# Three edits to one layer pair's kernel: first norm's root after the projections, small sums for the heads' norm, output projection begun during the retention's norm

## The reference

```
n = rms_norm(h, attn_norm_w)                 # per token: x * rsqrt(mean(x^2)+eps) * w
proj = n @ w_in                              # 1024 x 2816: aq 512, ak 128, av 128, rq, rk, rv, rg 512 each
aq = rope(rms_norm(aq per head of 64, q_norm_w)); ak = rope(rms_norm(ak per head, k_norm_w))
y_attn = windowed attention with a sink, |i-j| <= 128, 8 heads over 2 key heads
rq = rope(rq); rk = rope(rk) / 8
ret = bidirectional retention(rq, rk, rv)    # chunks of 128 tokens, decays forward and backward
y_ret = silu(rg) * rms_norm(ret per head of 64, ret_norm_w)
h = h + concat(y_attn, y_ret) @ w_out
h = h + (silu(m @ w_gate) * (m @ w_up)) @ w_down,  m = rms_norm(h)
```

## Time and profile before

| | |
|---|---|
| runs | 2897.14 us median of 3 (2895.31 to 2898.72) |
| the profiled execution | 2896.42 us, span of its instructions 2894.6 us |
| granted TensorE clock, mean | 0.986 |
| TensorE busy | 2768.2 us, 96% of the span |
| VectorE, ScalarE, GpSimd busy | 1606.4, 926.1, 1330.9 us |

### The profile page before, as it was taken

How to read it: one execution, slowest core, us unless ns; L and a number is a source line. 1 busy time by engine, 2 the same in 40 slices (tenths; PEclk the granted TensorE clock), 3 DMA queues, 4 the chain that set the end, 5 groups by cost and what they waited for, 6 DMA issues and landing times. The chain is left out here.

```text
span 2894.6 us, 36614 instructions
## 1 busy us (share of the span) xinstructions
PE 2768.2 (96%) x13748; PEld 2239.7 (77%) x13748; DVE 1606.4 (55%) x2419; ACT 926.1 (32%) x1793; POOL 1330.9 (46%) x1012
## 2 busy tenths in 40 slices
PE   5999989999999999999999899999899999999997
PEld 4777778778888888777766688878777788888886
DVE  7865665585555555542367742143368655555555
ACT  5655422232232222223334410021243322222222
POOL 3332332365656566543222234446613656566663
PEclk9999999999999999999999999999999999999999
DMA  3101001111111111131101011121201111111111
GB/s 123 37 30 37 30 20 75 50 44 55 52 60 54 48 55 52 44 117 37 37 30 38 30 37 56 53 113 62 66 23 44 48 59 55 48 55 51 59 51 66
DMA packets 71375, 151.94 MB, mean 52 GB/s; under 512 B 6448, under 2 KB 29360, under 8 KB 70064
## 3 DMA queue, kind: packets, MB, share of 16 engines
q1 hardware_dynamic: 64256, 123.76, 13.5%
q10 hardware_dynamic: 6960, 26.01, 2.3%
HBM read 141.36 MB, written 8.39 MB: 52 GB/s over the span
## 5 line engine op out<-in xcount | busy, mean ns | idle before, releaser
L603 POOL TENSOR_TENSOR WH<-WRAW,CST 128x512 fp32r<-128x512 f32 x204 | 228.1, 1118 | 896.5 <-PE PS L719 755.4
L717 PE MATMUL PS<-XH,WH 128*128 128x512 f32 x1248 | 514.7, 412 | 3.5 <-DVE XL L1994 2.8
L719 PE MATMUL PS<-XH,WL 128*128 128x512 f32 x1248 | 490.1, 393 | 0.0
L718 PE MATMUL PS<-XL,WH 128*128 128x512 f32 x1248 | 489.3, 392 | 0.0
L628 POOL TENSOR_TENSOR WL<-WRAW,WH 128x512 fp32r<-128x512 f32 x216 | 310.0, 1436 | 274.6 <-ACT WH L1622 273.6
L2377 DVE TENSOR_TENSOR H<-H,PS 128x512 f32<-128x512 f32 x352 | 235.8, 684 | 159.7 <-PE PS L1014 157.5
L717 PEld LDWEIGHTS PS<-XH,WH 128*128 128x128 f32 x1248 | 235.8, 189 | 85.7 <-issue 38.1
L1012 PE MATMUL PS<-HH,WH 128*128 128x512 f32 x704 | 275.0, 391 | 5.3 <-DVE HL L2311 5.3
L1622 ACT ACTIVATE WH<-WRAW 128x512 fp32r<-128x512 f32 x204 | 129.0, 632 | 471.5 <-PE PS L1014 383.1
L605 POOL TENSOR_TENSOR WL<-WRAW,WH 128x512 fp32r<-128x512 f32 x204 | 271.9, 1333 | 16.0
L719 PEld LDWEIGHTS PS<-XH,WL 128*128 128x128 f32 x1248 | 235.5, 189 | 51.6
(11 more groups left out here) (323 smaller groups left out, 5034.1 us busy)
## 6 DMA issues: line engine op xcount, KB each, us to landing
WRAW<-ws SPq DMA_DIRECT2D x104, 512.0 KB, 3.5
WRAW<-ws SPq DMA_DIRECT2D x176, 256.0 KB, 2.6
RAWX<-ws SPq DMA_DIRECT2D x88, 256.0 KB, 2.7
H<-xT ACTq DMA_DIRECT2D x4, 1024.0 KB, 10.9
H<-xT ACTq DMA_DIRECT2D x2, 2048.0 KB, 10.2
h_spill<-H ACTq DMA_DIRECT2D x1, 4096.0 KB, 11.8
H<-h_spill ACTq DMA_DIRECT2D x4, 1024.0 KB, 7.8
outT<-H ACTq DMA_DIRECT2D x4, 1024.0 KB, 4.4
```

Source lines behind the costliest of these rows:

```text
L603: pool.tensor_tensor(WH[:, j, c], WRAW[:, j, c], ONES[:, 0:1].to_broadcast((P, 512)), ALU.mult).then_inc(hi_split, 1)
L717: pe.matmul(out, WH[:, j, w], rh(kt), start=(n == 0), stop=False)
L718: pe.matmul(out, WH[:, j, w], rl(kt), start=False, stop=False)
L719: last = pe.matmul(out, WL[:, j, w], rh(kt), start=False, stop=(n == len(kts) - 1))
```

## The change

1. **First norm.** The input is no longer scaled by the inverse root ahead of the products. ScalarE rounds x times the gain at once (`x_highs`), VectorE makes the low part from x, gain and high part in one instruction (`x_lows`); the squares and sums stand between these. The root, inverse and spread of half 0 are asked for by TensorE inside the second half of `first_units`, those of half 1 behind it and inside slot 4. The spread inverse root is copied to SBUF (`RST`, in a part of RG not yet used), and VectorE's new `rooted1` multiplies each slot by it on the way from PSUM to `ACC`, and so frees the bank. `evacuate1` reads `ACC` in place of PSUM and no longer makes the scaled copy (the scale goes into `finish1`'s first instruction). `finish1`, and `after1` on both engines, run one slot later. In `first_units` the second unit lags three tiles behind in the first half too.
2. **Heads' norm.** `after1` on TensorE takes the squares as the stationary operand, 128 tokens at a time, and a 2-column matrix as the moving one: 4 products, result 128x8. Root and inverse work on 128x8; a new `spread1` (8 products of 128 moving columns) brings the inverse back to the heads' partitions in bank 6.
3. **Retention's norm.** The sums of the second half go into bank 4, spreads 0 to 3 alternate between banks 3 and 1 (so that a spread waits for the norm two before it, not one), and `r_sums(1)` and spreads 4 to 7 are issued inside the first half of the output projection's `first_units`, at tiles 2 and 6. ScalarE's `high` of tiles 0 to 3 go ahead of the second half's squares, the reload of x behind these; VectorE's inverse of half 1 goes behind the first half's `low`s.

```diff
-            for q in range(4):
+            act.wait_ge(vec_in, 32)
+            x_highs(0)
+            x_highs(1)
+            x_square(0)
+            x_square(1)
+            x_highs(2)
+            x_highs(3)
+            x_square(2)
+            norm_root(0, 0)
+            x_square(3)
+            nsq.n = 4
+            rst_copy(0)
...
-            norm_scale(0, V_N1)
+            x_lows(0)
+            x_lows(1)
+            x_sums(0)
+            x_sums(1)
+            x_lows(2)
+            x_lows(3)
+            x_sums(2)
+            norm_inverse(0, 0)
+            x_sums(3)
...
+                dve.tensor_tensor(ACC[:, g % 2], PS[:, bank], RST[h], ALU.mult).then_inc(free[bank], 1)
...
-                    pe.matmul(PS[:, MB], BD, XX[:, (g % 2) * HALF:(g % 2 + 1) * HALF], start=True, stop=True).then_inc(m_full, 1)
+                    for b in range(4):
+                        sq = XX[:, (g % 2) * HALF + b * P:(g % 2) * HALF + (b + 1) * P]
+                        last = pe.matmul(PS[:, MB, 2 * b:2 * b + 2], sq, BD[:, 0:P:64], start=True, stop=True)
...
+            def first_norm(h, kt):
+                if (h, kt) == (1, 0):
+                    norm_sums(0, 0)
+                if (h, kt) == (1, 3):
+                    norm_spread(0, 0)
+
+            def spread1(g):
+
+                pe.wait_ge(head_inv, g + 1)
+                if g:
+                    pe.wait_ge(proj_done, g)
+                for b in range(4):
+                    for hh in range(2):
+                        c = 60 + 8 * (g % 2) + 2 * b + hh
+                        last = pe.matmul(PS[64 * hh:64 * hh + 64, OB, blk(b)], STAT[:, c:c + 1].to_broadcast((P, 64)), IDENT,
+                                         start=True, stop=True)
...
-                    if done < g and (kt == 6 if g > 12 else kt == 7 or kt in (2, 5) and done < g - 1):
+                    if (g, kt) == (4, 2):
+                        norm_spread(0, 1)
+                    elif done < g - 1 and (kt == 6 if g > 12 else kt in (2, 5)):
                         after1(done)
                         done += 1
+                    elif kt in (4, 7) and spreads < min(done, 10):
+                        spread1(spreads)
+                        spreads += 1
...
-            r_sums(1)
-            for n in range(4, 8):
-                r_spreads(n)
...
+            def second_half(h, kt):
+
+                if (h, kt) == (0, 2):
+                    r_sums(1)
+                if (h, kt) == (0, 6):
+                    for n in range(4, 8):
+                        r_spreads(n)
...
-            for g in range(45):
-                if g:
+            for g in range(46):
+                if g == 2:
+                    norm_root(0, 1)
+                if 1 <= g < 45:
                     evacuate1(g - 1)
+                if g == 2:
+                    rst_copy(1)
...
-                if g:
-                    after1(g - 1)
+                if g >= 2:
+                    after1(g - 2)
...
+                if 1 <= g < 45:
+                    rooted1(g - 1)
                 if 0 <= s < 32:
                     soft1a(s)
-                if g:
-                    finish1(g - 1)
+                if g >= 2:
+                    finish1(g - 2)
```

More of the change, by code:

```diff
@@ L399, in prob @@
             return XX[:, 768 * (s % 2):768 * (s % 2) + 768].rearrange("p (a b) -> p a b", a=2)
+        RST = [RG[:, 3, half(h)] for h in range(2)]
+        PD, MF = [], []
+        for g in range(44):
+            PD.append((PD[-1] if PD else 0) + (KIND1[SLOTS1[g][0]] in "qkrR"))
+            MF.append((MF[-1] if MF else 0) + (KIND1[SLOTS1[g][0]] in "qkv"))
         def r_chunk(t):
@@ L745, in first_units @@
                                 norm_spread(k, 1)
+                            if between is not None and u == u0:
+                                between(h, kt)
                             j = u % 2
@@ L855, in after1 @@
                     nm.n += 1
-            first_units(0, XS_N1, 0)
-            done = 0
+            def first_norm(h, kt):
[12 more added lines that the diff above has]
+                                         start=True, stop=True)
+                last.then_inc(head_spread, 1)
+            first_units(0, XS_N1, between=first_norm)
+            norm_sums(0, 1)
+            done = spreads = 0
             for g in range(4, 44):
@@ L946, in r_sums @@
                         c = 8 * j + 2 * b
-                        last = pe.matmul(PS[:, 3, c:c + 2], r_squares(j)[:, blk(b)], BD[:, 0:P:64], start=True, stop=True)
+                        last = pe.matmul(PS[:, 3 + h, c:c + 2], r_squares(j)[:, blk(b)], BD[:, 0:P:64], start=True, stop=True)
                 last.then_inc(r_sum, 1)
@@ L1426, in _, with x_highs, x_square @@
             act.dma_start(ROPE[:], rope).then_inc(rope_in, 16)
-            for q in range(4):
+            def x_highs(q):
                 act.wait_ge(x_part[q], 16)
+                for i in range(4):
+                    kt, h = 4 * (q % 2) + i, half(q // 2)
+                    high(XH[:, kt, h], H[:, kt, h], v(V_N1 + kt))
+            def x_square(q):
                 if q >= 2:
@@ L1473, in evacuate1 @@
                         sc = scale if kind in "rR" else VEC[src, V_QN + (kind == "k"):V_QN + (kind == "k") + 1]
-                        last = act.activation(SQ[32 * r:32 * r + 32, p], PS[src, bank], ACT.Copy, scale=sc)
+                        last = act.activation(SQ[32 * r:32 * r + 32, p], ACC[src, p], ACT.Copy, scale=sc)
                     if kind in "qk":
                         last = act.activation(XX[:, p * HALF:(p + 1) * HALF], d, ACT.Square)
-                    last.then_inc(free[bank], 1)
+                    last.then_inc(turned_heads, 1)
             def after1(g):
@@ L2034, in _, with x_lows, x_sums @@
             dve.tensor_scalar(v(V_BGATE, 16), v(V_BGATE, 16), 0.5, None, ALU.mult).then_inc(vec_ready, 1)
-            for q in range(4):
+            def x_lows(q):
+                for i in range(4):
+                    kt, h = 4 * (q % 2) + i, half(q // 2)
+                    low(XL[:, kt, h], H[:, kt, h], XH[:, kt, h], v(V_N1 + kt))
+            def x_sums(q):
                 dve.wait_ge(squared, q + 1)
@@ L2043, in _, with rooted1 @@
                 dve.tensor_tensor(acc, a, sq[:, 1], ALU.add).then_inc(summed, 1)
-                if q % 2 == 0:
-                    dve.wait_ge(summed, q + 1)
-                if q == 2:
-                    norm_inverse(0, 0)
+            x_lows(0)
[7 more added lines that the diff above has]
+            x_sums(3)
             nsm.n = 4
-            norm_scale(0, V_N1)
             dve.wait_ge(rope_in, 16)
+            def rooted1(g):
+                u, h = SLOTS1[g]
+                bank = 2 * (u % 2) + h
+                dve.wait_ge(full[bank], uses[u][bank] + 1)
+                dve.wait_ge(rst_made, h + 1)
+                if g < 2:
+                    dve.wait_ge(col_sum, g + 1)
+                elif KIND1[SLOTS1[g - 2][0]] == "v":
+                    dve.wait_ge(m_full, MF[g - 2])
+                elif KIND1[SLOTS1[g - 2][0]] == "g":
+                    dve.wait_ge(gated, g - 2 - 2 * U_RG + 1)
+                else:
+                    dve.wait_ge(proj_done, PD[g - 2])
+                dve.tensor_tensor(ACC[:, g % 2], PS[:, bank], RST[h], ALU.mult).then_inc(free[bank], 1)
             def finish1(g):
```

125 lines of the change are left out of this document (60 added, 65 removed).

## The result

The changed kernel takes 2900.61 us (median of 20 runs, 2897.47 to 2906.27), the kernel before beside it on the same chip 2896.22 us (20 runs, 2893.71 to 2898.72). The ratio is 1.0017, 95% interval 1.001 to 1.0024: slower by 4.4 us, where 3.6 us less had been forecast. That is inside the 0.2% that I gave as "no change", but the interval lies wholly above 1 and the time outside the range of 2886 to 2900. The profiled execution took 2900.2 us against 2896.4, 3.8 us more.

What follows compares the result with a forecast made beforehand. TensorE was taken as the bound nearly everywhere, except gaps or half clock in the head, slots 4 and 5 (VectorE) and the retention's end. Terms 0.3+0.4-4.3 = -3.6 us on 2896.4 gave 2892.8, stated as 2893, range 2886 to 2900.

Steps and rivals of the forecast that it cites:

- no change: Whole kernel: a difference within about 0.2%, 5.8 us, is not told from no change; chance of "same" 0.57.
- Head: Start to slot 4: VectorE's chain has the inverse at 33.1 us, slot 4 starts at 44.9, not 53.5, gaining 8.6 us.
- Slots 4 to 11: The q and k slots: 73.7 us by dearer narrow products and waits for the root; first scores at 119.0 against 118.7.
- slots 7 to 11: Within the q and k slots: 5.48+1.87+0.7 = 8.1 us each, 40.5 together, with a 0.7 us wait each.
- slots 4 to 6: First q and k slots: 9.8, 11.4 and 12.0 us, with two sums and two spreads each in slots 5 and 6.
- Slots 12 to 43: Attention slots: `rooted1` adds 0.68 us per slot to VectorE but costs nothing; 0.7 in each of 32 if uncovered.
- Retention: One more VectorE gate instruction (0.7 us) ahead of the retention's first, partly seen by TensorE: 0.4 us worse (0 to 0.7).
- End of the retention: Second half's sums and spreads inside the output projection: 6.9 us saved at full clock, 1.3 if it falls, 4.3 taken.
- The clock is lost in the projections: Rival: narrow products and waits put a third of slots 5 to 11 at half clock, costing 9 us, 2902; chance 0.09.
- The overlap doesn't pay: Rival at the retention's end: half clock stays from 452 to 466 whatever is issued, 3.0 us less gain, 2896; chance 0.16.
- The chains are shorter: Rival: copies at 0.52 us, earlier head and full-clock overlap, all of it 2885 us; chance past the bound 0.34.

Runs made afterwards that it cites:

- e2: Changed kernel with the spreads of slots 7 to 11 asked at tile 7 only, not tile 4: 2897.92 us, ratio 0.9999 to the kernel before.
- e5: Changed kernel with the root ahead of the next slot's copies on ScalarE and, from slot 7, the spread at tile 7: 2893.06 us, ratio 0.9989 to before.
- e11: Changed kernel with root first, inverse ahead of the third rotation operation, spread at tile 7 from slot 7, last probabilities copy before last tanh: 2886.26 us, ratio 0.9964 to before.
- e6: Changed kernel with a constant 1.0 in place of the head norms' gain in the turned copies: 2898.17 us, ratio 1.0007 to the kernel before.
- e1: Changed kernel with the root of the slot before (and the first norm's second root copy) ahead of the next turned copies on ScalarE: 2894.06 us, ratio 0.9992 to before.
- e9: Changed kernel without the third part (retention's norm as before the change): 2904.32 us, ratio 1.0026 to the kernel before.
- e8: e5 plus the last copy of turned probabilities ahead of the last gate slot's tanh on ScalarE: 2891.22 us, ratio 0.9982 to the kernel before.
- e7: e1 plus the inverse ahead of the rotation's third operation on VectorE, spread still at tile 4: 2889.07 us, ratio 0.9974 to the kernel before.
- e4: Kernel before with the third part alone (retention's norm): 2893.04 us, ratio 0.9986 to the kernel before.
- e10: Changed kernel with the old heads' norm and the root ahead of the next slot's copies on ScalarE: 2897.94 us, ratio 1.0007 to the kernel before.
- e3: Changed kernel with the heads' norm as before (one block-matrix product, 128x512 roots and inverses, no spread): 2915.36 us, ratio 1.0062 to the kernel before.
- e12: e11 plus the head's spread of half 0 asked at tile 5, not 3, of the second half: 2884.39 us, ratio 0.996 to the kernel before.

## Why the prediction was wrong

**Head, -8.6 forecast, -10.8 measured.** The chain was the right one, and the low parts cost 0.67 each (0.66 taken). That the inverse was ready at 32.0 (33.1) is in part luck, as two terms miss and nearly cancel: the first low part began at 11.87 and not 10.4, behind ScalarE's table load, and GpSimd's turns cost 8.41-8x0.67 = 3.0 us and not 5.5. The rest of the difference is the 1.0 us for half clock, which this execution did not need; others with the same wait did (below).

**Slots 4 to 11, 73.7 forecast, 81.7 measured: this is the step that failed.** The step named the right wait, for the root behind "ScalarE's four turned copies", and priced it at 0.7 us. It was 1.16 to 1.56 us, and TensorE's own work was priced too low as well.

By terms, slots 7 to 11 (40.5 forecast, 44.0 measured) make 3.5 of the 8.0 us:

- TensorE's own slot is 7.65 us (seen without waits in e2, e5 and e11), not 5.48+1.87 = 7.35. The rows of narrow products, taken start to start, left out what lies between them and the next product: 0.3 in each of five slots, 1.5.
- The four waits are 5.5 us where I had five times 0.7: 2.0. The copies cost 0.73, not 0.62, which is 0.4 to 0.5 of the wait in slots 7 and 9; e6 shows 0.36 of it to be the factor per partition. In slots 8 and 10 the wait of 1.56 has a second cause of which the step had nothing: the inverse stands behind three VectorE operations while GpSimd splits. I had used exactly this turn-taking for the head and left it out of the next stage. The wait of 0.7 forecast in slot 11 did not come.

The other 4.5 are slots 4 to 6 (37.7, not 33.2):

- again 0.3 for each of five pairs of sum and spread, 1.5;
- 3.4 us at half clock in slot 5, worth 1.7;
- waits of 2.6 in slot 5 and 2.9 in slot 6, where the lengths forecast leave 2.2 and 2.8: 0.5;
- 0.8 that I cannot divide further, most of it in slot 4 (10.65 us, not 9.8).

The half clock began when TensorE had stood for 2.5 us. That it came from this is argued from the order, and from e1 and e5, which have neither the wait nor the low clock; it is not shown. The same two waits of 2.5 us were followed by half clock once here and twice in e2 and e9, and those of 2.1 us in e6 not at all. The window around it:

```profile
64.00:68.00 4.00, 3.80 (x21) 3.14 (x22) 1.87 (x4) 0.31 (x1) 0.18 (x1) 0.57 0.01 2
```

**Slots 12 to 43, nothing forecast, +1.3.** 0.86 of it is the wait before the last values, 1.55 and not 0.69 us: the tanh stands ahead of the last copy. I had not asked for the last slot what stands behind a waiting instruction in its queue; e8 and e11, in which the copy goes first, take it back. The other 0.45, which e11 keeps, is about the transposition that the forecast had put in front. That `rooted1` itself costs nothing in these 32 slots was right.

**Retention, +0.4 forecast, +1.8.** The gate instruction is there (0.4 by its 0.89 us and overlap). For the remainder I have only an argument, that the half clock fell in another place: 6.8 us of it between 436 and 443, where TensorE has no gap, against 3.4 us in that part before. In all this stage had less of it than before (clock 0.92 against 0.89). e9, with the same instructions up to there, took 62.2 us at the same 0.92. Over the fourteen profiled executions this stage lasts from 61.2 us at a mean clock of 0.97 (e7) to 66.6 at 0.85 (e8), though these two are the same in it but for when it begins, so 1.4 us here can't be put down to the change.

**End of the retention, -4.3 forecast, -5.3.** The direction was right; how much of it is work and how much clock can be told only in part. Here are windows from the first spread to the loop, one line each of the kernel before, of e9 (both without the third part) and of e1 (with it):

```profile
437.62:488.21 50.59, 45.98 (x364) 40.32 (x361) 27.94 (x42) 15.72 (x29) 4.89 (x5) 0.87 0.21 84
```

```profile
446.52:496.02 49.50, 44.89 (x364) 39.24 (x360) 27.93 (x42) 15.72 (x29) 4.88 (x5) 0.90 0.22 86
```

```profile
441.71:490.11 48.40, 45.59 (x364) 38.08 (x360) 27.85 (x42) 16.05 (x29) 4.89 (x5) 0.89 0.22 88
```

At a clock of 0.89 to 0.90 the third part is worth 49.50 - 48.40 = 1.1 us. The changed kernel ran this stretch at 0.96 and in 45.28 us, like e4, e7, e10 and e11; e6 took 46.81 at 0.93; e1, e2, e3, e5, e8 and e12 took 48.4 at 0.89. Between the kernel before and e9 (13.7 and 10.2 us at half clock) a microsecond at half clock costs 0.32 us, with the third part 0.45 to 0.47. Carried on to the 3.4 us of the changed kernel this makes the moved work 2.0 us there, an estimate from two executions. So of the 5.3 us some 1.1 to 2.0 are the moved work, and the rest a higher granted clock than before's 0.87.

Five of the twelve profiled executions with the third part had the 0.96, neither of the two without it. That the third part raises the clock would fit the 3.2 to 4.1 us by which the medians differ, but it is not shown, and the clock of the whole execution, which is on record for every run, speaks against it: on average 0.9858 in e4 (11 runs) and 0.9860 in the kernel before beside it (28), 0.9856 in the changed kernel (20) and 0.9858 in e9 (11). A difference of 0.0002 is 1.2 us at half clock, and so some 0.6 us of time, an estimate. Where the rest of those 3.2 to 4.1 us comes from stays open. The Trainium skill, "TensorE: Matmul & The Clock Gate", A second HAM failure mode, tells of a clock that goes to and fro with short idle times between groups of matmuls; the rows here agree in that equal programs ran this stretch at 0.89 and at 0.96, but none shows that the short waits bring it.

**The rivals.** "The clock is lost in the projections" named the right sign and nearly the right time, 2902, by the wrong mechanism, so by luck: the half clock in slots 4 to 11 is 3.4 us, not 19, and worth about 1.7, and the same slots had 6.8 us of it before. The loss against the forecast was waits and the narrow products' price. "The overlap doesn't pay" failed too, with 5.3 us gained in its stage. "The chains are shorter" was the opposite of the truth. No rival said that the chains are longer, though the copies' ceiling of 0.68 and GpSimd's turns were both in my rows.

## What to carry to other kernels

When a change lets one engine depend on another inside a loop with a hand-written order, write down for each small instruction what stands ahead of it in its queue, and put the short ones that others wait for (a root of eight columns, their inverse) ahead of the long ones that can wait: here one instruction of 0.25 us and one of 0.20 us, moved (e7), took eight slots from 81.7 to 69.6 us. Of these 12.1 us about 1.1 belong to a copy of 0.6 us that moved with the first, and 1.7 to half clock that this execution did not have. Follow each chain once around the loop: one that closes on itself can set the period, as in e3, though no engine is full. And price a small instruction by what it adds to the loop, not by its own length: here 2.17 us for a pair whose rows show 0.95 and 1.09. An effect that is priced in one stage, such as two engines that take turns, has to be carried through all stages in which both work.

## What the runs showed of the hardware

- A ScalarE copy of 32x512 out of SBUF takes 0.73 us with a factor per partition and 0.64 us with a constant one (four in 2.92 and in 2.55, changed kernel and e6); out of PSUM, with the factor, 0.68. So the factor cost 0.09 us, and the copy out of SBUF was 0.05 dearer than that out of PSUM, where I had assumed it cheaper.
- While GpSimd ran its 128x512 splits (1.04 to 1.61 us), VectorE's three operations of 0.74, 0.69 and 0.69 us took 1.09, 1.77 and 1.41 us in slots 8 and 10: together twice the time. `rooted1`, with one operand in SBUF and one in PSUM, took 0.69 us at 89.47 as without a split. The inverse of e3, one operand in and one out, took 3.35 us beside a split too, as everywhere else. The Trainium skill, "SBUF — State Buffer", Who interferes with whom, says that a VectorE instruction with two inputs from SBUF contends with a GpSimd instruction that reads SBUF, and that one with at most one, outside VectorE's two-port modes, doesn't; the trace agrees.
- The same wait of 2.7 us in the head was followed by half clock in seven of the eleven profiled executions that have it (e1, e3, e5, e6, e7, e9, e10) and not in the other four (the changed kernel, e2, e8, e11). The window of e7 from 12 us to slot 4:

```profile
12.00:44.43 32.43, 28.83 (x120) 22.45 (x121) 23.03 (x28) 22.14 (x28) 8.16 (x7) 0.95 0.34 128
```

  Against 30.73 us at 1.00 in the changed kernel (the first window above), this is 1.7 us more, with VectorE's inverse within 0.1 us of the same time (31.91 and 31.80). In e12, without the wait, the clock was 1.00.
- A spread (eight products, 16 passes) and a head sum (four products of two columns, 8 passes) show 1.09 and 0.95 us, but cost a slot 7.65 - 5.48 = 2.17 us, more than both together.
